# A two-layer block on one core: the place of a 128x128 multiply in VectorE's attention step, and projections that run two tiles behind their gates

## The reference, cut to what matters

```python
h = rms_norm_2(x, norm_g[l]) * (1.0 + scale) + shift        # 512 tokens; hc: 256 context tokens
o_na = neighbourhood_attention(...)                          # 8 heads of 64
o_wa = window_attention(axial_rope(...), axial_rope(...), ...)   # 8 query heads, 2 kv heads, with a sink
y_a = conv_branch(a_glu, a_gate, ...)
y_b = (o_na * silu(n_gate)) @ w_proj_b
y_c = (o_wa * silu(w_gate)) @ w_proj_c
y = sigmoid(g_a) * y_a + sigmoid(g_b) * y_b + sigmoid(g_c) * y_c
x = x + gate * (y @ w_o)
```

## Time and profile before

| | us |
|---|---|
| median of 3 runs (lowest to highest) | 4239.12 (4237.78 to 4239.26) |
| the profiled execution, its own time | 4233.64 |
| its span | 4232.4 |
| PE busy | 3804.8 (90%) |
| DVE busy | 2278.7 (54%) |
| ACT busy | 1474.5 (35%) |
| POOL busy | 1208.2 (29%) |
| PE clock granted, mean | 0.957 of full |

### The profile page before, as it was taken

The page is one execution under the profiler, slowest core; times in us unless marked ns, Lnnn a source line. Parts: engine busy times, 40 slices in busy tenths (PEclk is TensorE's granted clock), DMA queues, the critical chain, the costliest instruction groups (busy, mean ns, idle before and its releaser), DMA issues. The chain is left out here.

```text
span 4232.4 us, 54199 instructions
## 1 busy us (share of the span) xinstructions
PE 3804.8 (90%) x21364; PEld 3150.4 (74%) x21364; DVE 2278.7 (54%) x3704; ACT 1474.5 (35%) x2516; POOL 1208.2 (29%) x793
## 2 busy tenths in 40 slices
PE   5999768889999999898999799889999989789989
PEld 4888646778888888747888687578877867568767
DVE  6555684567556777645533689721155339730442
ACT  3223433444224323444422322432234222443442
POOL 1112434234014201304201324813211324514214
PEclk9999889999999999999999899899999999999999
DMA  7565214335564555312332311102110212102102
GB/s 264 172 200 150 98 44 169 110 125 162 174 190 147 177 186 166 117 35 96 129 94 85 118 50 49 37 26 70 45 51 11 68 38 84 56 27 94 65 23 92
DMA packets 131595, 433.12 MB, mean 102 GB/s; under 512 B 14480, under 2 KB 14480, under 8 KB 130704
## 3 DMA queue, kind: packets, MB, share of 16 engines
q1 hardware_dynamic: 130912, 427.04, 31.1%
q10 hardware_dynamic: 432, 2.62, 0.2%
HBM read 427.51 MB, written 2.10 MB: 102 GB/s over the span
## 5 line engine op out<-in xcount | busy, mean ns | idle before, releaser
L603 PE MATMUL ps<-cut 128*128 128x512 f32 (+1 forms) x5216 | 1873.5, 359 | 191.6 <-POOL cut L532 48.3
L604 PE MATMUL ps<-cut 128*128 128x512 f32 (+1 forms) x5216 | 1834.1, 352 | 0.0
L605 PE MATMUL ps<-cut 128*128 128x512 f32 (+1 forms) x5216 | 1831.5, 351 | 0.0
L603 PEld LDWEIGHTS ps<-cut 128*128 128x128 f32 x5216 | 1011.8, 194 | 350.5 <-issue 127.7
L604 PEld LDWEIGHTS ps<-cut 128*128 128x128 f32 x5216 | 1013.3, 194 | 131.3 <-issue 6.4
L605 PEld LDWEIGHTS ps<-cut 128*128 128x128 f32 x5216 | 1011.9, 194 | 125.9
L532 POOL TENSOR_TENSOR cut<-cut 128x1024 fp32r<-128x1024 f32 (+3 forms) x334 | 735.3, 2205 | 1224.7 <-ACT cut L522 1224.0
L522 ACT ACTIVATE cut<-cut 128x1024 fp32r<-128x1024 f32 (+3 forms) x680 | 630.9, 936 | 578.8 <-PE ps L605 473.0
L532 DVE TENSOR_TENSOR cut<-cut 128x1024 fp32r<-128x1024 f32 (+2 forms) x346 | 420.8, 1218 | 447.2 <-ACT cut L522 447.0
L871 POOL TENSOR_TENSOR cut<-cut 128x512 fp32r<-128x512 f32 (+1 forms) x100 | 136.9, 1369 | 1012.8 <-ACT cut L831 1012.8
L2055 DVE SCALAR_TENSOR_TENSOR cut<-cut,cols 128x512 f32<-128x512 f32 (+1 forms) x330 | 280.5, 850 | 11.7
(11 more groups left out here) (289 smaller groups left out, 3974.0 us busy)
## 6 DMA issues: line engine op xcount, KB each, us to landing
cut<-in_ffn_in SPq DMA_DIRECT2D x200, 512.0 KB, 4.0
cut<-in_mod_w SPq DMA_DIRECT2D x128, 512.0 KB, 4.3
cut<-in_ffn_out SPq DMA_DIRECT2D x96, 384.0 KB, 3.3
cut<-in_ffn_out SPq DMA_DIRECT2D x96, 320.0 KB, 3.0
cut<-in_w_ada SPq DMA_DIRECT2D x48, 512.0 KB, 3.6
cut<-in_w_merge SPq DMA_DIRECT2D x48, 512.0 KB, 3.5
cut<-in_even_in SPq DMA_DIRECT2D x36, 512.0 KB, 3.5
cut<-in_proj SPq DMA_DIRECT2D x48, 256.0 KB, 2.6
```

The lines of the kernel that those rows point to most:

```text
L603: te.matmul(o, hi[:, k - ka, w], xs[0], start=k == 0, stop=False)
L604: te.matmul(o, hi[:, k - ka, w], xs[1], start=False, stop=False)
L605: ins = te.matmul(o, lo[:, k - ka, w], xs[0], start=False, stop=last)
```

## The change

In `dve_pairs` the multiply of job i-4's output moves from the end of step i to its beginning, ahead of job i's maxima. `MERGES` becomes merge 0, 1, then merge m and proj m-2 for m = 2 to 7, then proj 6 and 7. The sigmoids get three buffers in place of two (wait for the share m-3 in place of m-2). Before the window attention the merges run up to proj 4; step 0 then holds merge 7 and proj 5, step 1 proj 6, step 2 proj 7. The ropes of queries 2 and 3 both come behind proj 4, and PE waits for the last of them, `v_rp (l, 3)`, before step 0.

```diff
-MERGES = [("merge", 0)] + [x for m in range(1, 8) for x in (("merge", m), ("proj", m - 1))] + [("proj", 7)]
+MERGES = [("merge", 0), ("merge", 1)] + [x for m in range(2, 8) for x in (("merge", m), ("proj", m - 2))] + [("proj", 6), ("proj", 7)]
...
+    SGM = [[t512[i] for i in (11, 12, 13)], [t512[14][:, 0:256], t512[14][:, 256:512], t512[10][:, 256:512]]]
...
     def dve_pairs(tag, jobs, mid, clear=()):
         n = len(jobs)
         for i in range(n + 4):
+            if i >= 4:
+                o = jobs[i - 4]["out"]
+                ve.wait_ge(*(yield "a_av", tag, i - 4))
+                ve.tensor_tensor(o, o, PS[bank["p_pv", tag, i - 4]][:, 128:256], ALU.mult).then_inc(*sig("v_o", tag, i - 4))
             if i < n:
...
-            if i >= 4:
-                o = jobs[i - 4]["out"]
-                ve.wait_ge(*(yield "a_av", tag, i - 4))
-                ve.tensor_tensor(o, o, PS[bank["p_pv", tag, i - 4]][:, 128:256], ALU.mult).then_inc(*sig("v_o", tag, i - 4))
             yield from mid(i)
...
-                    n, s = g[1] - g[0], 11 + 2 * gi + m % 2
+                    n, s = g[1] - g[0], SGM[gi][m % 3]
...
-                    if m >= 2:
-                        se.wait_ge(*(yield "v_y0", l, i, m - 2, gi) if i == 0 else (yield "v_y", l, i, m - 2, gi))
+                    if m >= 3:
+                        se.wait_ge(*(yield "v_y0", l, i, m - 3, gi) if i == 0 else (yield "v_y", l, i, m - 3, gi))
...
+    ROPES = {2: (0,), 3: (1,), 4: (2, 3)}
...
-            if m in (2, 3, 4, 5):
-                yield from pe_rope((l, m - 2), WQ[:, m - 2, 0:512], ("v_hn", ("wq", l), m - 2, 0), 512, con("rax"))
+            for t in ROPES.get(m, ()):
+                yield from pe_rope((l, t), WQ[:, t, 0:512], ("v_hn", ("wq", l), t, 0), 512, con("rax"))
...
-        yield from merge(MERGES[:-3])
-        te.wait_ge(*(yield "v_rp", (l, 4)))
+        yield from merge(MERGES[:-4])
+        te.wait_ge(*(yield "v_rp", (l, 3)))
         yield from pe_pairs(("wa", l), wa_jobs(l), at_step({
-            0: lambda: merge(MERGES[-3:-2]), 1: lambda: merge(MERGES[-2:-1]), 2: lambda: merge(MERGES[-1:]),
+            0: lambda: merge(MERGES[-4:-2]), 1: lambda: merge(MERGES[-2:-1]), 2: lambda: merge(MERGES[-1:]),
```

More of the change, by code:

```diff
@@ L2184, in epilogue @@
                 for gi, g in enumerate(groups):
-                    n, s = g[1] - g[0], 11 + 2 * gi + m % 2
+                    n, s = g[1] - g[0], SGM[gi][m % 3]
                     if gi == 0:
                         se.wait_ge(*(yield "p_mm", ("merge", l, i, m), 0))
-                    if m >= 2:
-                        se.wait_ge(*(yield "v_y0", l, i, m - 2, gi) if i == 0 else (yield "v_y", l, i, m - 2, gi))
-                    se.activation(t512[s][:, 0:n], PS[bank[("merge", l, i, m), 0, gi]][:, 0:n], ACT.Sigmoid).then_inc(*sig("a_sg", l, i, m, gi))
+                    if m >= 3:
+                        se.wait_ge(*(yield "v_y0", l, i, m - 3, gi) if i == 0 else (yield "v_y", l, i, m - 3, gi))
+                    se.activation(s[:, 0:n], PS[bank[("merge", l, i, m), 0, gi]][:, 0:n], ACT.Sigmoid).then_inc(*sig("a_sg", l, i, m, gi))
             yield from act_linear((kind, l, i, m), epilogue if kind == "merge" else nothing)
@@ L2198, in epilogue @@
                 for gi, g in enumerate(groups):
-                    n, s = g[1] - g[0], 11 + 2 * gi + m % 2
-                    tb, yt = t512[s][:, 0:n], Y[:, m, g[0]:g[1]]
+                    n = g[1] - g[0]
+                    tb, yt = SGM[gi][m % 3][:, 0:n], Y[:, m, g[0]:g[1]]
                     if gi == 0:
@@ L2491, in beside @@
                 yield from dve_rope((l, 4), WK[:, 0, 0:512], 512, con("cosx"), con("sinx"), t512[2], t512[3])
-            if m in (2, 3, 4, 5):
-                yield from dve_rope((l, m - 2), WQ[:, m - 2, 0:512], 512, con("cosx"), con("sinx"), t512[2], t512[3])
+            for t in ROPES.get(m, ()):
+                yield from dve_rope((l, t), WQ[:, t, 0:512], 512, con("cosx"), con("sinx"), t512[2], t512[3])
         def merge(items):
             return dve_merge(l, 1, QG, items, beside)
-        yield from merge(MERGES[:-3])
+        yield from merge(MERGES[:-4])
         yield from dve_pairs(("wa", l), wa_jobs(l), at_step({
-            0: lambda: merge(MERGES[-3:-2]), 1: lambda: merge(MERGES[-2:-1]), 2: lambda: merge(MERGES[-1:])}),
+            0: lambda: merge(MERGES[-4:-2]), 1: lambda: merge(MERGES[-2:-1]), 2: lambda: merge(MERGES[-1:])}),
             [("v_y", l, 1, m, len(QG) - 1) for m in (6, 7)])
```

## The result

The changed kernel takes 4245.94 us (median of 20 runs, 4236.49 to 4252.13) against 4239.09 us (20 runs, 4231.88 to 4245.08): ratio 1.0016, 95% interval 1.001 to 1.0023, so 7 us or 0.16% slower. Forecast were 4242.5 us and "no measurable change"; the time lies inside the range. The interval doesn't hold 1, so the change is measurably slower, by less than the 0.2% that the forecast called no change. The profiled execution has a span of 4242.2 us against 4232.4, at a granted clock of 0.953 against 0.957.

What follows compares the result with a forecast made beforehand. PE is busy nine tenths of the span; its largest second-block wait is for the multiply, 56.2 us. -13.8 +3.2 +10.0 +4.0 = +3.4 us, about 4237, plus 5.5 to the runs' median: 4242.5 us, range 4227 to 4254.

Steps and rivals of the forecast that it cites:

- Part 1: Multiply first in DVE's step: PE's wait for it goes, but DVE and ACT take turns; attention stages sum to -13.8 us.
- na 0: -1.1: Neighborhood attention, layer 0: entry -1.0, steady part +1.8, exit -1.9, together -1.1 us.
- Part 2: Three gates before branch 0's first share: PE starts later by 1.6 us in each layer, +3.2 us.
- Part 3: Before window attention PE waits for two ropes behind proj 4: +5.4 us in layer 0, +4.6 in layer 1.
- Part 4: Half clock after the new stalls before window attention: 2.0 us each, +4.0 us together (between 0 and 5.5).
- A: Rival: the stop before window attention is hidden, Part 3 and Part 4 give nothing; -10.6 us, 4228.5; chance 0.14.
- B: Rival: PE's wait for the multiply just goes, ACT's copy always in time; -39 us, 4200; chance 0.08.
- C: Rival: PE's stops cost full price, 7.1+6.0 and 5.5 us, plus half clock behind first shares; +8.0, 4250.5; chance 0.20.
- D: Rival: PE at half clock becomes slowest in layer 1's attention stages, which gain nothing; +18.5 us, 4261; chance 0.06.

## Why the prediction was right, and where it was wrong

*Part 1, taking turns: right.* L1809 waits for ACT L1800 in 75 of 80 jobs, and the spacings came out within 0.06 us of the forecast, in na, layer 0, only for the second six jobs. The gain in layer 1 (-7.2 and -11.3; measured -6.0 and -11.4) and the loss in wa, layer 0 (+5.8; measured +6.2) are there. The experiments with the multiply elsewhere show the cause: with the multiply behind the negation VectorE's front no longer stands behind ScalarE's last copy, and layer 0 loses nothing.

*Part 1, "na 0: -1.1": mis-sized.* It measured +4.7 with the multiply alone and +3.7 in the whole change. The step that failed is the one that takes the fronts at 2.36 and 1.02 us, as they stood in the trace of before, where the 24 negations of this stage exceeded 0.17 us by only 0.22 us in all. In a turn a front counts with everything that delays it, and in this stage the negation meets GpSimd's work: with the multiply first alone the excess is 3.8 us, and in the changed kernel 4.3, of which 0.54 us in each of two light jobs and 1.63 in one. With ScalarE negating, the stage is 5.1 us shorter, 160.56 us, 0.4 below the kernel before and so within 0.7 of my -1.1. The six jobs without such a meeting took 27.67 us, to the forecast 27.7. The turn isn't needed for it: the orders alone, with the multiply last, had 3.0 us of it too. What remains of the 5.8 us, between 0.7 and 2.2, I can't name.

The Trainium skill (SBUF — State Buffer, "SBUF: two separate sides") says that the port pair that VectorE and GpSimd share is an exclusive lock, which a VectorE instruction needs in a two-port mode or with two SBUF inputs, and which the one that starts first keeps for its whole instruction. Of the two-port mode it says (VectorE: DVE Perf Modes, "What auto-detection actually checks") that a single-source operation between SBUF tensors of even size takes it, if that mode is enabled for the operation. The traces agree on the negation, which is such an operation and takes up to 2.25 us, ending with the subtraction; the maxima (one of two inputs in PSUM) and the copy (PSUM) are not held. The reciprocal has the same shape and one source in SBUF and isn't held either; whether the mode isn't enabled for it no run here shows. The cause that the runs show is that the negation waits for GpSimd's subtraction; that a lock does it is the page's account. I had used a rule of this kind for the ropes and not looked for which small instruction in the turn it also covers.

*Part 2, three gates first: right.* 11.30 and 10.37 us of wait (forecast 11.3 and 10.4), ended by a split of 2.34 us, and 1.5 us less wait in each layer when it is undone (1.6).

*Part 3, the wait for the last rope: right.* 4.82 and 4.03 us against 5.4 and 4.6. In layer 0 proj 4's epilogue took 2.31 us (3119.64 to 3121.95) and the ropes 4.13 (to 3126.08), as taken; PE came to the wait 0.6 us later than I had it, since its rope products, row L1499, took 1.88 us (from 3119.44). I had taken 1.3, the distance to the next product's start; the row itself had 1.88 before, too.

*Part 4, the clock: right in size.* 4.3 us against 4.0. Parts 3 and 4 were forecast at 14.0 together; the experiment without the stop found 14.7 in the profile and 16.5 by the ratios.

*The sum.* By stages -6.5, +3.1 and +14.7 make +11.3; the profiled executions differ by 9.8; the medians by 6.9. The forecast was +3.4. Between the profiled executions it missed by 6.4 us, about the size of the na 0 term; that it came within 3.5 us of the difference of the medians is luck. By the ratios the multiply alone gained 10.6 us, less than the 13.8 forecast, and the orders on top of it took 17.4 (forecast 17.2), but alone only 11.0, so the agreement of 17.4 with 17.2 shows little.

*The rivals.* A, the stop is hidden: out, nothing came back. B, the wait just goes: out, since the multiply alone gained 10.6 us and not 39, and 39 us of its waits came back at ACT's copies. C, full price of the stops: the waits were shorter than forecast (8.9 and not 10.0 us), the half clock behind them cost 4.3 us, and the half clock behind branch 0's long waits lasted 8.5 us in both layers together against 9.0 before, so there is no added stretch. The ratios alone (16.5 us, give or take 5) wouldn't rule out C's 18.6. Its condition was also reckoned wrong: the stops would have to cost 5.1 us more than I counted, not 4.3, to pass 8.5 us from no change. D, layer 1's gain lost: out, the gain is there (-6.0 and -11.4).

## What to carry to other kernels

When an instruction is moved to the front of an engine's step, look at what it waits for and at who waits behind it. If it waits for the end of another engine's step, which itself starts behind this engine's front, both engines take turns, and the period is front plus step plus handover, however little work either has. The place that paid was the earliest one at which the awaited result is there anyway: first in the step gave 11 us, behind the negation 36, in the middle of the maxima 50. That place can differ from job to job: in wa, layer 0, with its light jobs, behind the negation was better than between the maxima by 5.5 us. Moving a 0.17 us negation off VectorE gave 12 us more with the multiply first, and with it between the maxima 8, less than the intervals resolve. A row in a list of waits doesn't tell what removing it gains: 48.6 of 56.2 us went, 39.0 us of wait appeared at another row, and the kernel was 11 us faster.

## What the runs showed of the hardware

A VectorE TENSOR_SCALAR from SBUF to SBUF over 128x2 elements took 0.17 us in 64 of 80 cases and up to 2.25 us beside GpSimd's 128x1024 subtraction (2.35 us; the kernel with the multiply first alone), while RECIPROCAL over the same 128x2 elements kept its 0.16 us beside one. In the twelve kernels in which VectorE negates, 75 negations started inside such a subtraction; all but the two that started in its last 0.1 us ended within 0.05 us of its end. The smallest instruction of the step was the one that a neighbour's big one could hold.

Idle times of PE of 4.82 and 4.03 us were followed by half clock, 3.3 and 5.3 us long: the shorter stop had the longer stretch of half clock behind it.
